# Weighing with the values ahead of the third part of a step's fill, in a two-layer hybrid decoder step

## The chip, the cores and the metric

The kernel runs on one core of a Trainium2 chip. The metric is the device time of one execution in microseconds (us). TensorE is called PE here, VectorE DVE, ScalarE ACT, GpSimd POOL and SyncE SP. Each engine works off its own instructions in order, and they wait for one another through semaphores.

## What is computed

One step of a decoder trunk with two layers, for a prompt of 1024 rows and 8 sample rows of width 1024. Per layer, cut to what matters here:

```python
h = rms_norm(x, norm1_g);  proj = h @ w_in          # columns: pool 512 | q 512 | k 512 | v 512
q, k = rope(q), rope(k)                             # 4 heads, two components of 64 each; v is 128 wide
s = einsum(q, k) * 64 ** -0.5                       # two score matrices a head, causal
p = softmax(s);  a = p[0] - lam * p[1]
o = einsum(a, v)                                    # 'weighing with the values'
attn = rms_norm(o, subln_g) * (1 - lam_init)
x = x + concat(pool_mixer(u), attn) @ w_out
x = x + conv_gated_ffn(rms_norm(x, norm2_g))
```

The 8 sample rows attend to 1024 cached positions each, in pages that a table names, and to their own key and value. A last RMS norm gives the outputs; new keys, values and states are stored as well.

## The kernel before

Activations lie transposed, features on the partitions, 1032 columns (1024 prompt rows and 8 sample rows) in three tiles of 344. A large product is made of three matmuls per 128 x 128 block (high part times high part, low times high, high times low). PSUM has eight banks; `claim(pe, name, b)` makes PE wait until the last use of bank b has been freed, and `freed(eng, name)` makes an engine wait for the freeing of one named use.

The attention of a layer is a loop over four heads (L725), and each head has eight steps (L734), one per block of 128 query rows, in the order 7, 0, 6, 1, 5, 2, 4, 3 (`ORDER`). Step s of a head holds, on PE:

- `scores` of the next step (L556 to L562), into banks 2 to 5; DVE reduces them to maxima (`maxima`, L1842), ACT takes two exponentials (`exps`, L1327 and L1330), and DVE forms their weighted difference (`combine`, L1850 to L1858), whose products have tiny ones (L1850, L1853: one element per partition) and one wide one (L1856).
- `turn_p` (L570), one or two rounds: the step's weights are transposed into bank 6, and ACT copies them to `a_T` (`take_p`, L1345).
- the fill: matmuls of a large product that are cut into portions. In heads 0 to 2 it is the projection of the next head's k, q and v (L477), nine slices of 24 matmuls, and `FILL` says how many matmuls a step holds; in head 3, the fourth, it is the output projection (L495) in slices of 21, with `FILL_OUT`. A step's fill comes in three parts (`part` matmuls twice, then the rest); in step 0 of head 3 the whole fill is the third part. The fill's slices go to banks 0 and 1 in turn. ACT copies a finished slice out (`take_k`, `take_q`, `take_v`, L1241), and behind the last slice of k or q it issues four DMAs that swap halves for the rotation (`rotate`, L1257). The slice that ends in a step's third part is copied late in ACT's step. The last slice of q ends with the sixth of the eight matmuls of step 4's third part.
- `turn_out` of the step before (L592): the normalised output rows are transposed, through bank 6.
- special work: step 0 turns the values (banks 7 and 6), step 4 turns the sample rows' scores (L614, L618; banks 7, 6, 7) and in heads 0 to 2 the next head's keys (`turn_k`, L531; banks 6 and 7, copied by ACT in `store_k`, L1290), step 5 forms the sample weights (L624, bank 6, behind a softmax of ACT, L1372, and DVE's `soft_weights`, L1904 to L1907), steps 6 and 7 weigh the sample rows' value pages (`sample_values`, L638, bank 7, copied by ACT, L1380); step 7 of heads 0 to 2 also spreads the next head's sample queries over the partitions (L542, bank 6). In step 7 `sample_out` (L646 to L649) sums the sample rows' output in a bank of the fill's ring.
- `weigh` (L581): two passes for each block of weights, into bank 7. It waits for bank 7, and for ACT's copies of the transposed weights.

Behind `weigh`, ACT takes squares of the rows (`square`, L1339; for the sample rows L1336), POOL adds and takes the reciprocal root (`rms`, L1024 and L1026), DVE multiplies (`normalise`, L1868), and frees bank 7. These three stand near the beginning of the next step in their engines' order: ACT's `square` of a step stands behind the slice copies of that step's third part.

POOL also splits weights into their low parts (`split_lo`, L1006), issues the gathers of the cached pages (L1041) and multiplies the cached keys by the query (`k_product`, L1049), three at a time in steps 1 and 2; its `rms` of step 0 stands ahead of the three products of step 1. DVE sums these products (L1883). In head 3, step 0, ACT, DVE and POOL split the seven chunks of the mixed rows, for which the output projection waits.

Behind the heads each layer runs its feed-forward network (L810 and L833), which the change does not touch.

Of the kernel before, what the change touches and what calls it, by code (L numbers as in the profile page):

```python
# [62 lines left out]
def rounds(i):  # L63
    return [list(range(a, min(a + 4, i + 1))) for a in range(0, i + 1, 4)]


def third(s, counts):

    return 0 if counts is FILL_OUT and s == 0 else counts[s] // 3
# [66 lines left out]
def hybrid_decoder_kernel(nc, x_prompt, x_sample, cache_k, cache_v, state_pool, state_conv, page_table, norm1_g, w_in,  # L136
# [4 lines left out]
    with ExitStack() as ctx:  # L141
# [177 lines left out]
        def claim(pe, name, b):  # L319
            USE[name] = (b, USES[b])  # L320
            if USES[b]:
                pe.wait_ge(bank_free[b], USES[b])
            USES[b] += 1
            return b
# [10 lines left out]
        def freed(eng, name):  # L335
            b, n = USE[name]
            eng.wait_ge(bank_free[b], n + 1)
# [71 lines left out]
        def _(pe):  # L409
# [96 lines left out]
            def slices(l, items, banks):  # L506
                for kind, n, t in items:
                    yield from (in_slice if kind == "in" else out_slice)(l, n, t, next(banks))

            def take(fill, n):  # L510
                for _ in range(n):
                    next(fill, None)
# [21 lines left out]
            def small_k(it):  # L534
                b = claim(pe, ("ks", it), 6)
                pe.transpose(bank[0:8, b, 0:P], k_buf[it % 2][:, SEQ:T], ident).then_inc(bank_full[b], 1)
# [8 lines left out]
            def scores(it, s):  # L545
                i = ORDER[s]
                q, k = q_buf[it % 2], k_buf[it % 2]
                for c in range(2):
                    claim(pe, ("s", it, s, c), 2 + 2 * c)
                if s == 0:  # L550
                    pe.wait_ge(roped, it * 2 + 2)
                halves = [(2 + 2 * c, slice(c * HEAD_DIM, (c + 1) * HEAD_DIM)) for c in range(2)]
                for n, at in enumerate(range(0, i * P, 512)):
                    w = min(512, i * P - at)
                    for b, rows in halves:
                        pe.matmul(bank[:, b + n, 0:w], q[rows, i * P:(i + 1) * P], k[rows, at:at + w],  # L556
                                  start=True, stop=True)
                last = [bank[:, b + i // 4, (i % 4) * P:(i % 4 + 1) * P] for b, _ in halves]
                for c, (b, rows) in enumerate(halves):
                    pe.matmul(last[c], q[rows, i * P:(i + 1) * P], k[rows, i * P:(i + 1) * P], start=True, stop=False)  # L560
                for c, (b, rows) in enumerate(halves):
                    pe.matmul(last[c], mask[:, 0, :], mask[:, 1, :], start=False, stop=True  # L562
                              ).then_inc(bank_full[b], 1)

            def turn_p(it, s, r):
                b = claim(pe, ("p", it, s, r), 6)
                if r == 0:
                    freed(pe, ("s", it, s, 1))
                for n, i in enumerate(rounds(ORDER[s])[r]):
                    ins = pe.transpose(bank[:, b, n * P:(n + 1) * P], probs[s % 2][:, i * P:(i + 1) * P], ident)  # L570
                ins.then_inc(bank_full[b], 1)

            def weigh(it, s):
                b = claim(pe, ("o", it, s), 7)
                i = ORDER[s]
                if s == 0:
                    freed(pe, ("vt", it, 1))
                for r, blocks in enumerate(rounds(i)):
                    freed(pe, ("p", it, s, r))
                    for n, j in enumerate(blocks):  # L580
                        ins = pe.matmul(bank[:, b, 0:P], a_T[:, r, n * P:(n + 1) * P], v_tok[:, j, :],  # L581
                                        start=(j == 0), stop=(j == i))
                ins.then_inc(bank_full[b], 1)

            def turn_out(it, n):
                b = claim(pe, ("to", it, n), 6)
                if n == QT_N:
                    freed(pe, ("so", it))
                    pe.transpose(bank[:, b, 0:8], o_norm8, ident[0:8, 0:8]).then_inc(bank_full[b], 1)
                else:  # L590
                    freed(pe, ("o", it, n))
                    pe.transpose(bank[:, b, 0:P], o_norm, ident).then_inc(bank_full[b], 1)  # L592

            def turn_v(it, r, b):
                claim(pe, ("vt", it, r), b)
                l, h = it // N_HEADS, it % N_HEADS
                if r == 0:
                    freed(pe, ("g", l, U_V(h), NT - 1))
                for a in range(4):
                    i = 4 * r + a  # L600
                    ins = pe.transpose(bank[:, b, a * P:(a + 1) * P], v_T[:, i * P:(i + 1) * P], ident)
                ins.then_inc(bank_full[b], 1)

            def small_v(it):
                b = claim(pe, ("vs", it), 6)
                pe.transpose(bank[0:16, b, 0:P], v_T[:, SEQ:T + 8], ident).then_inc(bank_full[b], 1)

            def turn_sample_scores(it):
                for r in range(2):
                    b = claim(pe, ("ss", it, r), 7 - r)  # L610
                    if r == 0:
                        pe.wait_ge(k_red, (it + 1) * DEC_BATCH)
                    for a in range(4):
                        ins = pe.transpose(bank[0:16, b, a * P:(a + 1) * P], s_score[:, :, :, 4 * r + a], ident)  # L614
                    ins.then_inc(bank_full[b], 1)
                b = claim(pe, ("ss", it, 2), 7)
                pe.wait_ge(qk_done, it + 1)
                pe.matmul(bank[0:16, b, 0:1], comp8, ones[:, 0:1], start=True, stop=True).then_inc(bank_full[b], 1)  # L618
# [45 lines left out]
            for l in range(DEPTH):  # L664
# [47 lines left out]
                it = l * N_HEADS  # L712
# [12 lines left out]
                for h in range(N_HEADS):  # L725
                    it = l * N_HEADS + h
                    final = h == N_HEADS - 1
                    if final:
                        fill = slices(l, [("out", m, t) for m in range(KC) for t in range(NT)], banks)
                        counts = FILL_OUT  # L730
                    else:
                        fill = slices(l, [("in", u(h + 1), t) for u in (U_K, U_Q, U_V) for t in range(NT)], banks)
                        counts = FILL
                    for s in range(QT_N):  # L734
                        part = third(s, counts)
                        if s + 1 < QT_N:
                            scores(it, s + 1)
                        elif not final:
                            scores(it + 1, 0)
                        turn_p(it, s, 0)  # L740
                        take(fill, part)
                        if len(rounds(ORDER[s])) > 1:
                            turn_p(it, s, 1)
                        take(fill, part)
                        if s >= 1:
                            turn_out(it, s - 1)
                        elif h:
                            turn_out(it - 1, QT_N - 1)
                        if s == 0:
                            turn_v(it, 0, 7)  # L750
                            turn_v(it, 1, 6)
                            small_v(it)
                            if h:
                                turn_out(it - 1, QT_N)
                        if s == 4:
                            turn_sample_scores(it)
                            if not final:
                                turn_k(it + 1, 0, 6)
                                turn_k(it + 1, 1, 7)
                        if s == 5:  # L760
                            sample_weights(it)
                        if s in (6, 7):
                            sample_values(it, s - 6)
                        if s == 7 and not final:
                            spread_q(it + 1, 0, 6)
                            spread_q(it + 1, 1, 6)
                            small_k(it + 1)
                        take(fill, counts[s] - 2 * part)
                        if s == 7:
                            sample_out(it, next(banks))  # L770
                        weigh(it, s)


                it = l * N_HEADS + N_HEADS - 1
# [1356 lines left out]
```

## Time and profile before

| | us |
|---|---|
| median of 3 runs | 2887.01 (2886.06 to 2888.28) |
| the profiled execution | 2887.58 |
| its span, first to last instruction | 2885.7 |
| PE busy | 2596.9 (90%) |
| DVE busy | 1535.2 (53%) |
| POOL busy | 820.8 (28%) |
| ACT busy | 744.3 (26%) |
| chain that ended last: PE L810 and L833 (feed-forward) | 33% and 18% |
| chain: PE L477 and L495 (the fills, and the projections ahead of the heads) | 5% and 5% |

The granted clock of PE is 0.941 of full speed over the span. Times below are counted from the first instruction of the profiled execution. In brackets behind a row of a timeline stands how long the engine was idle before it, and which engine's which line ended that.

### The profile page before, as it was taken

What the parts mean: (1) busy time and instruction counts of PE and PEld (TensorE: products, weight loads), DVE (VectorE), ACT (ScalarE), POOL (GpSimd) and SP (SyncE); (2) the same over time, 40 slices, a digit from 0 to 9 for tenths busy, and PEclk for the clock granted to TensorE, in tenths of its full rate; (3) what the DMA queues carried; (4) which work ended last, traced back from release to release, by engine and by line L of the source; (5) the groups of instructions that cost most, each with busy time, mean ns of one, the idle gap of its engine ahead of it and who ended that gap; (6) DMA issues with size and microseconds to landing.
All of it is one profiled execution on the core that took longest, in us unless ns stands there. A gap on an engine that the chain in (4) does not pass through costs nothing.

```text
span 2885.7 us, 41322 instructions
## 1 busy us (share of the span) xinstructions
PE 2596.9 (90%) x16556; PEld 2424.5 (84%) x16556; DVE 1535.2 (53%) x1903; ACT 744.3 (26%) x1409; POOL 820.8 (28%) x543
## 2 busy tenths in 40 slices
PE   6888777898999999999987888869899999999996
PEld 5777766888999999999886766758799999999996
DVE  5564764545445545455564664743654444554545
ACT  3223333232111121111132333332421111112112
POOL 1243553422222222222121553553222222222220
PEclk8889888999999999999998889889999999999997
DMA  3323344211111111111112343342011111111101
GB/s 122 121 93 120 109 139 132 90 45 45 44 44 44 48 52 47 44 45 51 47 55 89 106 144 117 106 138 89 29 45 44 44 44 44 44 47 50 50 30 59
DMA packets 78360, 205.96 MB, mean 71 GB/s; under 512 B 9146, under 2 KB 31100, under 8 KB 77994
## 3 DMA queue, kind: packets, MB, share of 16 engines
q1 hardware_dynamic: 35230, 112.92, 11.5%
q0 software_dynamic: 18496, 67.58, 7.2%
q10 hardware_dynamic: 24540, 24.15, 2.9%
q8 instruction: 67, 1.10, 0.2%
q14 instruction: 27, 0.22, 0.0%
HBM read 176.63 MB, written 19.98 MB: 68 GB/s over the span
## 4 chain that ended last, share of the span: by engine, by line
PE 72%; DVE 15%; ACT 5%; issue 2%; DMA 2%; POOL 2%; ACTq 1%; DVEq 0%; POOLq 0%
PE bank L810 33%; PE bank L833 18%; PE bank L477 5%; PE bank L495 5%; DVE stat L1850 4%; PE bank L581 2%; DVE parts_b L1883 1%; PE bank L638 1%; DVE stat L1842 1%; DMA arena<-in_cache_v,idx 1%; PE bank L556 1%; DVE arena L1702 1%; DVE arena L1856 1%; PE bank L862 1%; DVE arena L1810 1%
## 5 line engine op out<-in xcount | busy, mean ns | idle before, releaser
L1128 POOL TENSOR_TENSOR w_lo<-w_raw,w_hi 128x1024 fp32r<-128x1024 f32 x126 | 310.1, 2461 | 1157.4 <-ACT w_hi L1538 1157.4
L2040 DVE TENSOR_TENSOR resid<-bank,resid 128x1032 f32<-128x1032 f32 x336 | 414.2, 1233 | 91.7 <-PE bank L833 91.7
L810 PE MATMUL bank<-act_hi,w_hi 128*128 128x344 f32 x2016 | 433.6, 323 | 0.0
L810 PE MATMUL bank<-act_hi,w_lo 128*128 128x344 f32 x2016 | 427.6, 320 | 0.0
L810 PE MATMUL bank<-act_lo,w_hi 128*128 128x344 f32 x2016 | 426.5, 320 | 0.0
L810 PEld LDWEIGHTS bank<-act_hi,w_lo 128*128 128x128 f32 x2016 | 340.9, 189 | 0.0
L810 PEld LDWEIGHTS bank<-act_hi,w_hi 128*128 128x128 f32 x2016 | 336.1, 189 | 3.7
L810 PEld LDWEIGHTS bank<-act_lo,w_hi 128*128 128x128 f32 x2016 | 338.0, 188 | 0.0
L477 PE MATMUL bank<-act_hi,w_hi 128*128 128x344 f32 x672 | 236.6, 352 | 10.3 <-DVE arena L1791 10.3
L1006 POOL TENSOR_TENSOR w_lo<-w_raw,w_hi 128x1024 fp32r<-128x1024 f32 (+1 forms) x56 | 134.6, 2405 | 381.9 <-ACT w_hi L1167 381.7
L833 PE MATMUL bank<-gate_hi,w_hi 128*128 128x344 f32 x1008 | 235.6, 342 | 0.0
L477 PE MATMUL bank<-act_hi,w_lo 128*128 128x344 f32 x672 | 234.7, 349 | 0.0
L477 PE MATMUL bank<-act_lo,w_hi 128*128 128x344 f32 x672 | 229.4, 341 | 0.0
L833 PE MATMUL bank<-gate_hi,w_lo 128*128 128x344 f32 x1008 | 213.4, 320 | 0.0
L833 PE MATMUL bank<-gate_lo,w_hi 128*128 128x344 f32 x1008 | 213.2, 320 | 0.0
L1842 DVE TENSOR_REDUCE stat<-bank 128x1 f32<-128x128 f32 (+7 forms) x128 | 90.8, 751 | 228.0 <-PE bank L562 224.8
L833 PEld LDWEIGHTS bank<-gate_hi,w_hi 128*128 128x128 f32 x1008 | 154.7, 188 | 36.0 <-DVE resid L2040 24.1
L1550 ACT ACTIVATE arena<-arena 128x1024 f32<-128x1024 f32 x44 | 46.7, 1062 | 525.0 <-DVE arena L2023 525.0
L833 PEld LDWEIGHTS bank<-gate_hi,w_lo 128*128 128x128 f32 x1008 | 169.2, 188 | 0.0
L833 PEld LDWEIGHTS bank<-gate_lo,w_hi 128*128 128x128 f32 x1008 | 169.1, 188 | 0.0
L2031 DVE TENSOR_TENSOR arena<-bank,arena 128x1032 f32<-128x1032 f32 x44 | 54.3, 1234 | 207.4 <-PE bank L810 207.2
L2006 DVE COPY arena<-bank 128x16 f32<-128x16 f32 x44 | 7.7, 176 | 284.4 <-PE bank L817 284.3
(240 smaller groups left out, 4406.8 us busy)
## 6 DMA issues: line engine op xcount, KB each, us to landing
w_raw<-in_w_up SPq DMA_DIRECT2D x88, 512.0 KB
w_raw<-in_w_down SPq DMA_DIRECT2D x44, 512.0 KB
w_raw<-in_w_in SPq DMA_DIRECT2D x32, 512.0 KB
arena<-arena ACTq DMA_DIRECT2D x64, 129.0 KB, 2.6
out<-arena ACTq DMA_DIRECT2D x16, 512.0 KB, 3.2
w_raw<-in_w_out SPq DMA_DIRECT2D x16, 448.0 KB
mix_spill<-arena ACTq DMA_DIRECT2D x12, 516.0 KB, 3.1
w_raw<-mix_spill SPq DMA_DIRECT2D x12, 516.0 KB
```

The lines of the kernel that those rows point to most:

```text
L477: ins = pe.matmul(bank[:, b, 0:TW], w_of(w, l, n, k), x[:, k, cols(t)], start=(k == 0 and m == 0), stop=(k == KC - 1 and m == 2))
L495: ins = pe.matmul(bank[:, b, 0:TW], w_of(w, l, U_O + m, c), x[:, c, cols(t)], start=(c == 0 and a == 0), stop=(c == KC - 2 and a == 2))
L581: ins = pe.matmul(bank[:, b, 0:P], a_T[:, r, n * P:(n + 1) * P], v_tok[:, j, :], start=(j == 0), stop=(j == i))
L810: ins = pe.matmul(grp(u[0])[:, t, :], w_of(w, l, n, k), x[:, k, cols(t)], start=(k == 0 and n_ == 0), stop=(k == KC - 1 and n_ == 2))
L833: ins = pe.matmul(grp(u[0])[:, t, :], w_of(w, l, n, m), x[:, cols(t)], start=(n_ == 0), stop=(n_ == 2))
L1006: pool.tensor_tensor(w_lo[:, slot, 0:width], w_raw[:, r % SLOTS, 0:width], w_hi[:, slot, 0:width].bitcast(F32), ALU.subtract).then_inc(w_l ...
L1128: pool.tensor_tensor(w_lo[:, slot, :], w_raw[:, r % SLOTS, 0:1024], w_hi[:, slot, :].bitcast(F32), ALU.subtract).then_inc(w_lo_done, 1)
L1550: act.activation(gate[:, 0:SEQ], conv_c[:, 0:SEQ], ACT.Silu)
L1842: dve.tensor_reduce(stat[:, s % 2, c:c + 1], flat(b)[:, 0:width], AX_X, ALU.min).then_inc(att_bias, 1)
L1850: step(dve.tensor_tensor(st[:, 2:3], st[:, 4:5], neg_lam[it // N_HEADS], ALU.mult))
L2031: dve.tensor_tensor(tiles(gate), grp(u[0]), tiles(gate), ALU.mult).then_inc(fg_free[u[0]], 1)
L2040: dve.tensor_tensor(tiles(resid[:, m, :]), grp(u[0]), tiles(resid[:, m, :]), ALU.add).then_inc(fg_free[u[0]], 1)
```

## The change

In the loop over the steps, PE's call of `weigh` moves from behind the third part of the fill (and, in step 7, behind `sample_out`) to ahead of it. No other engine's order changes.

```diff
                             spread_q(it + 1, 0, 6)
                             spread_q(it + 1, 1, 6)
                             small_k(it + 1)
+                        weigh(it, s)
                         take(fill, counts[s] - 2 * part)
                         if s == 7:
                             sample_out(it, next(banks))
-                        weigh(it, s)
```

## Rows read from the trace of the kernel before

**Rows 1.** Page, chain that ended last: shares of the span by engine
```profile
PE 72%; DVE 15%; ACT 5%; issue 2%; DMA 2%; POOL 2%; ACTq 1%; DVEq 0%; POOLq 0%
```
**Rows 2.** Line L581 (weigh): what its engine's idle time before it waited for (us, times)
```profile
  issue: 1.8, 8
```
**Rows 3.** Chain of waits in the second head (286 to 345): start, us, what
```profile
289.18 5.80 DVE stat L1850
...
331.59 0.61 ACT arena L1290
...
333.97 0.35 ACT arena L1241
334.41 0.51 ACTq L1257
...
337.78 0.87 ACT arena L1327 x2
```
**Rows 4.** Timeline of POOL, second head, steps 0 and 1: start, us, engine, line
```profile
283.57 2.35 POOL L1006 TENSOR_TENSOR w_lo<-w_raw,w_hi 128x1024 fp32r<-128x1024 f32 x1 [5.61 <-ACT w_hi L1167]
285.87 0.20 POOL L1024 TENSOR_TENSOR stat<-stat 128x1 f32<-128x1 f32 x1
...
287.93 7.03 POOL L1049 TENSOR_TENSOR arena<-arena 128x1024 f32<-128x1024 f32 x3
```
**Rows 5.** Timeline of PE, second head: end of step 1, step 4, step 5
```profile
296.59 0.76 PE L556 MATMUL bank<-arena 64*128 64x128 f32 x4 [3.62 <-DVE arena L1856]
...
333.65 1.77 PE L581 MATMUL bank<-arena 128*128 128x128 f32 x12
...
341.62 0.91 PE L624 MATMUL bank<-small,arena 16*128 16x8 f32 x7 [1.11 <-DVE small L1907]
```
**Rows 6.** Timeline of PE, second head, step 7
```profile
364.90 3.59 PE L638 MATMUL bank<-arena 128*1 128x128 f32 x64 [3.12 <-DMA arena<-in_cache_v,idx]
...
370.23 1.12 PE L542 MATMUL bank<-arena,con 128*128 128x512 f32 x2 [0.69 <-ACT arena L1320]
...
372.47 0.32 PE L477 MATMUL bank<-act_hi,w_hi 128*128 128x344 f32 x1
...
373.09 0.31 PE L477 MATMUL bank<-act_hi,w_lo 128*128 128x344 f32 x1
...
374.33 1.16 PE L581 MATMUL bank<-arena 128*128 128x128 f32 x8
```
**Rows 7.** Timeline of ACT, second head, step 6
```profile
354.06 0.28 ACT L1380 ACTIVATE con<-bank 128x128 f32<-128x128 f32 x1 [1.58 <-PE bank L638]
```
**Rows 8.** Timeline of POOL, second head, steps 6 and 7
```profile
354.30 1.68 POOL L1041 DMA_INDIRECT arena<-in_cache_v,idx  x1 [5.26 <-PE bank L638]
...
375.98 0.18 POOL L1024 TENSOR_TENSOR stat<-stat 128x1 f32<-128x1 f32 x1 [2.46 <-ACT arena L1339]
```
**Rows 9.** Timeline of ACT, first head, step 4
```profile
230.71 0.60 ACT L1290 ACTIVATE arena<-bank 128x512 f32<-128x512 f32 x1 [0.26 <-PE bank L531]
...
232.99 0.43 ACT L1241 ACTIVATE arena<-bank 128x344 f32<-128x344 f32 x1
```
**Rows 10.** Timeline of PE, first head, step 4
```profile
232.34 1.50 PE L581 MATMUL bank<-arena 128*128 128x128 f32 x12
```
**Rows 11.** Timeline of PE, fourth head, steps 0 and 1
```profile
486.70 0.62 PE L495 MATMUL bank<-act_hi,w_hi 128*128 128x344 f32 x1 [2.73 <-DVE act_lo L1919]
...
498.95 3.15 PE L581 MATMUL bank<-arena 128*128 128x128 f32 x16
...
514.23 0.66 PE L495 MATMUL bank<-act_hi,w_hi 128*128 128x344 f32 x1 [6.31 <-DVE resid L1913]
```
**Rows 12.** Timeline of DVE, fourth head, step 1
```profile
506.28 5.91 DVE L1850 TENSOR_TENSOR stat<-stat,lam 128x1 f32<-128x1 f32 x1
```
**Rows 13.** Stretches: busy us (count) of PE, PEld, DVE, ACT, POOL; granted clock; DMA
```profile
228.40:231.80 3.40, 3.10 (x13) 3.10 (x14) 1.21 (x1) 1.49 (x4) 0.00 (x0) 0.50 0.02 5
324.00:334.20 10.20, 6.93 (x30) 5.85 (x31) 4.29 (x10) 5.76 (x14) 1.27 (x2) 0.50 0.25 79
```

## Prediction: what the change does to the time

> **What bounds the kernel now.** I read the chain that ended last, by engine: 72% of it is PE, 15% DVE, 5% ACT [rows 1]. The change touches the eight heads' steps alone, so I then read the matmul of the weighing by its source line: PE sat idle before it for 1.8 us in all, in 8 places [rows 2]. The weighing waits for nothing today, so nothing can be won at its own place; what an earlier one gives must come through its readers (ACT's square, POOL's root, DVE's normalising), and what it costs through what it meets sooner.
>
> The chain inside one head (the second of the first layer) shows two stretches that set the pace. At the end of step 1 DVE's one-element product L1850 lasts 5.80 us [rows 3]; it ends with POOL's three products of cached keys (L1049, from 287.93 for 7.03 us) [rows 4], and PE meanwhile waits 3.62 us for the next scores [rows 5]. In steps 4 and 5 the chain is ACT's: the second copy of turned keys (L1290), later the copy of q's last slice (L1241), four DMA issues that rotate q (L1257), the exponentials (L1327), then DVE, then PE's sample weights (L624) at 341.62, for which PE has stood 1.11 us [rows 5].
>
> **The change part by part.** No instruction is added or removed. In 64 steps the third part of the fill (6 to 12 matmuls in a layer's first three heads, 18 to 26 in its fourth) and the weighing trade places, so PE's work is the same and only waits move.
>
> *The weighing's two waits, met sooner.* It needs ACT's copy of the turned weights out of bank 6, and bank 7. turn_out, which stands ahead of it in both kernels, claims bank 6 and so has waited for that copy; in the first head of a layer, at step 0, the turned values do the same. Cost nothing. Bank 7 was last used by the previous weighing, whose normalising turn_out also waits for: nothing in steps 1, 2, 3 and 5. In step 0 the small turn of the values has waited for the last copy out of both banks; in step 7 of the first three heads two later copies by ACT lie between. Three places are left where bank 7 has just been filled: step 4 (the keys of the next head, in the fourth head the sample scores), step 6 (the sample values), and step 7 of the fourth head.
>
> *Step 4 of the first three heads: the stall.* PE's last turn of keys ends as ACT's L1290 starts at 331.59; that ends 0.61 later, at 332.20 [rows 3]. PE, which now runs eight fill matmuls there, would stand until some 332.25: 0.7 us. The same pattern (PE, a 512-wide copy by ACT, PE on the same bank) stands in step 7 with 0.69 us [rows 6]. Queued behind the weighing on PE are those eight fill matmuls, and ACT waits for the sixth of them.
>
> *Step 4: the late slice.* ACT now takes q's last slice at 333.97, right behind its softmax, because PE had finished it under that cover. Afterwards the fill comes behind stall and weighing. Second head: PE is at its lower clock level (granted 0.50, which is 1.2 GHz) until 334.2 [rows 13]; a pass of the weighing takes 3.15/16 = 0.197 us there [rows 11] and 1.50/12 = 0.125 at the upper level [rows 10]. From 332.25, ten passes end at 334.2 and two more at 334.45. The sixth fill matmul starts 5 x 0.155 later (four starts from 372.47 to 373.09, [rows 6]) and lasts 0.32, so ACT starts at 335.6, 1.6 us late. The four issues and the exponentials follow back to back on ACT, with 0.1 us of slack to PE's own turns: 1.5 us at L624. First head: bank free at 230.71 + 0.60 = 231.31 [rows 9]; the lower level ends at 231.8 [rows 13]; so the weighing ends at about 233.05 and the slice at 234.15, where ACT took it at 232.99: 1.2 us. Three heads have the long stretch of lower clock, three the short one: 3 x 1.5 + 3 x 1.2 = 8.1 us. Bounds: nothing, if the sample weights are held by something else; and 0.7 + 1.77 = 2.5 us a head (the stall and the whole weighing [rows 5]), 15 us. I take 8.1, because the chain of the trace runs through this very copy. It is not given back in the head: L624 is what PE waits for, and what follows is timed from it.
>
> *Step 6, first three heads.* PE ends the sample values when ACT's copy L1380 starts, 354.06, for 0.28 us [rows 7]: a stall of 0.4 us. But POOL issues the last four value pages from the end of the same matmuls (354.30, [rows 8]), and PE then waits 3.12 us for them in step 7 [rows 6]. The 0.4 goes into that wait: nothing; if this cover were gone, 6 x 0.4 = 2.4 us.
>
> *Fourth heads.* Step 6 and step 7 have the same stall with no page wait behind: 0.4 each. Step 4 waits for a copy of one column behind a 512-wide one: between 0.4 and 0.7, I take 0.6. Sum 1.4 a layer, 2.8 us; bounds 0 and 4. In step 0 the weighing moves ahead of 18 fill matmuls that wait for chunks of the mixed rows: its 3.15 us go into the wait of 2.73 us ahead of the first of them and the next one [rows 11]. PE then reaches the next scores some 3 us sooner, but waits again until 514.23, 6.31 us today [rows 11], for DVE, whose L1850 again lasts 5.91 us [rows 12] under POOL's products. POOL's chain there starts from its own splitting of weights, not from the square. Gain nothing.
>
> *The gains through the square.* In step 0 POOL's root starts at 285.87, while its own splitting of weights (283.57 + 2.35 = 285.92) ends [rows 4]; behind steps 1, 2 and 3 it likewise follows POOL's preceding instruction at once. An earlier square waits there. POOL does stand idle for the square behind step 4, but there the square follows ACT's DMA issues and not the weighing [rows 3], and behind step 7 (375.98, 2.46 us idle [rows 8]). In step 7 the weighing comes sooner by eight fill matmuls and the sample's sum, but on ACT the square stands behind the copy of the last value slice, which the weighing's 1.16 us [rows 6] now delays. Net 0.2 us a head, 4 heads that it helps (in the fourth heads step 0 is bound by the turned weights): 0.8 us.
>
> Sum: 8.1 + 2.8 - 0.8 = +10.1 us. The profiled execution took 2887.58 us (span 2885.7); 2897.7 on that footing. The median of the runs, 2887.01, lies 0.57 lower: 2897.1.
>
> One rule of the Trainium skill speaks otherwise. SBUF — State Buffer, Who interferes with whom, says that a VectorE instruction with two SBUF inputs and a GpSimd one that reads SBUF exclude each other for one whole instruction, and that the order of issue decides. The trace agrees on the exclusion, but L1850 outlasts three POOL products (5.80 us against 7.03/3 = 2.34 each). By the trace's form the fourth heads gain nothing; by the rule's they could, which is the third rival.
>
> **Rivals.**
> 1. *The wait is hidden after all.* L624 waits 1.11 us in the second head; if it were held by the softmax's sum and not by the late slice, the 0.7 us stall would drown in it. For: that wait exists [rows 5]. Against: the chain passes through L1241. Time: 2887.0 + 2.8 - 0.8 = 2889.0.
> 2. *The clock falls more often.* Each head's step 4 or 5 holds a stretch at 1.2 GHz today [rows 13], after PE had stood still; longer waits may add one per head. A stretch of 3.4 us at half pace loses 1.7 us: 6 x 1.7 on top, 2907.3. For: L624's wait grows to about 2 us. Against: fill follows at once.
> 3. *Not slower: DVE gets ahead of POOL in the fourth heads.* The scores of step 2 come 3 us sooner there; if that lets DVE's L1850 and the products behind it pass before POOL's three, PE's wait of 6.31 us goes, in two layers: 10.1 - 12.6 = -2.5, 2884.5. It decides if the sums of ACT's exponentials reach DVE before POOL starts, which it does some time before L1850's 506.28 [rows 12]. Against: DVE's reductions of those scores and both exponentials must still come first, and the first product alone is not enough.
> 4. *The root does start sooner*, because the square is what holds POOL: ten fill matmuls, 1.55 us, off the wait behind step 1 of six heads: 10.1 - 9.3 = 0.8, 2887.8. Against: POOL has no idle time before it [rows 4].
>
> That the change does nothing is excluded: the order of instructions on PE is written out by hand.
>
> **How the numbers follow.** Chances: forecast 0.62 (its own range 2892 to 2902), rival 1 0.17, rival 2 0.11, rival 3 0.06, rival 4 0.04. What this kernel's measurement can tell from no change is about 0.2%, 5.8 us: faster is below 2881.2, slower above 2892.8. Slower: the forecast without its lowest edge and rival 2, 0.70. Same: rivals 1, most of 3 and 4, and that edge, 0.23. Faster: rival 3 with more than two waits saved, or a chain I have not seen, 0.07. The range runs from 2887.5, just under rival 1, to 2904, short of rival 2's full price.
>
> **What would show it.** Right: in step 4 a new wait of about 0.7 us before L581 on ACT's L1290; L1241 in that step directly behind the fill and not behind the softmax; L624's wait up from 1.11 to about 2 us; a 0.4 us wait before L581 in step 6, and L638's 3.12 us shorter by as much; L1850 still 5.8 us. Wrong: no wait at L581, L624 unmoved against the turned keys, or a shorter L1850 in the fourth heads.

## The result, and the profile after

The changed kernel took 2906.36 us (median of 4 runs, 2903.36 to 2910.96) beside 2886.53 us for the kernel before (4 runs, 2884.08 to 2888.28): a ratio of 1.0071, 95% interval 1.0053 to 1.0088, or +15 to +25 us. It is slower, as forecast, but by about twice the +10.1 us that the sum gave. A second measurement (the repeat among the experiments) gave 1.0048, interval 1.0029 to 1.0067, or +8 to +19 us. The profiled execution after took 2905.41 us; its span is 2903.5, where before it was 2885.7: +17.8.

The chain of the profile after, shares by engine, against [rows 1]: TensorE's share falls by two points and "issue" takes three.

```profile
PE 70%; DVE 15%; issue 5%; ACT 4%; POOL 2%; DMA 2%; ACTq 1%; DVEq 0%; POOLq 0%
```

First, what the weighing (L581) waits for now, from TensorE's waits in the kernel after (engine, line, what it waited for: us in total, times, longest). Of before there was nothing to wait for [rows 2].

```profile
PE bank L638 <- DMA arena<-in_cache_v,idx: 17.0, 6, 3.3
...
PE bank L624 <- DVE small L1907: 15.2, 8, 2.2
...
PE bank L581 <- ACT arena L1290: 4.1, 6, 0.7
...
PE bank L581 <- ACT con L1380: 3.2, 8, 0.4
...
PE bank L581 <- ACT arena L1368: 1.2, 2, 0.6
...
PE bank L581 <- ACT parts_b L1380: 0.8, 2, 0.4
```

The same view of the kernel before has, of these, only the two that are not the weighing's:

```profile
PE bank L638 <- DMA arena<-in_cache_v,idx: 17.5, 6, 3.6
...
PE bank L624 <- DVE small L1907: 12.3, 8, 2.3
```

The four new waits are 9.3 us, each in the place and of the size that was forecast (0.69, 0.40, 0.6, 0.4 us). So the stalls are not where the forecast fell short.

Second, step 4 of the first and the second head on TensorE, after (start, us, line, idle before it and what ended it), to be held against [rows 5, 10]:

```profile
230.79 2.93 PE L581 MATMUL bank<-arena 128*128 128x128 f32 x12 [0.69 <-ACT arena L1290]
243.03 1.92 PE L624 MATMUL bank<-small,arena 16*128 16x8 f32 x16 [1.93 <-DVE small L1907]
...
335.49 2.93 PE L581 MATMUL bank<-arena 128*128 128x128 f32 x12 [0.69 <-ACT arena L1290]
...
347.00 2.06 PE L624 MATMUL bank<-small,arena 16*128 16x8 f32 x16 [2.19 <-DVE small L1907]
```

The twelve matmuls of the weighing last 2.93 us where they lasted 1.50 and 1.77 us. ScalarE in the same two places, against [rows 3, 9]:

```profile
230.14 0.60 ACT L1290 ACTIVATE arena<-bank 128x512 f32<-128x512 f32 x1 [0.26 <-PE bank L531]
...
235.47 0.46 ACT L1241 ACTIVATE arena<-bank 128x344 f32<-128x344 f32 x1 [2.96 <-PE bank L477]
...
334.84 0.60 ACT L1290 ACTIVATE arena<-bank 128x512 f32<-128x512 f32 x1 [0.26 <-PE bank L531]
...
339.44 0.46 ACT L1241 ACTIVATE arena<-bank 128x344 f32<-128x344 f32 x1 [2.23 <-PE bank L477]
```

From the end of L1290 to the copy of q's last slice (L1241) it is now 4.73 and 4.00 us; before it was 232.99 - 231.31 = 1.68 and 333.97 - 332.20 = 1.77 us. ScalarE now waits for the fill (L477), as the forecast said.

Third, the length of the place. I measured it from the end of L1290 to the first L624, in the first three heads of both layers: six stretches. The view of stretches gives for each the busy time of PE, PEld, DVE, ACT and POOL, then the granted clock and the DMA share; the last line sums the six. Before:

```profile
231.31:240.54 9.23, 7.62 (x53) 6.66 (x52) 3.85 (x11) 4.25 (x11) 0.74 (x2) 0.97 0.44 114
332.19:341.63 9.44, 8.33 (x53) 7.36 (x52) 3.82 (x11) 4.44 (x11) 0.73 (x2) 0.89 0.43 112
...
sum 57.82, PE 48.60 PEld 42.82 DVE 23.07 ACT 25.77 POOL 4.42; mean PE 8.10 PEld 7.14 DVE 3.85 ACT 4.29 POOL 0.74
```

And after:

```profile
230.73:243.03 12.30, 10.32 (x54) 9.09 (x55) 3.86 (x11) 4.37 (x12) 0.74 (x2) 0.79 0.33 86
335.43:347.00 11.57, 9.33 (x55) 8.27 (x55) 3.86 (x11) 4.37 (x12) 0.73 (x2) 0.87 0.35 91
...
sum 72.07, PE 59.71 PEld 52.73 DVE 23.17 ACT 26.22 POOL 4.42; mean PE 9.95 PEld 8.79 DVE 3.86 ACT 4.37 POOL 0.74
...
225.80:235.90 10.10, 8.88 (x39) 7.21 (x36) 1.73 (x3) 4.46 (x9) 0.00 (x0) 0.50 0.18 54
```

The six places are 72.07 - 57.82 = 14.25 us longer, for which the forecast had 8.1. Of these, 11.1 us is busy time of TensorE (59.71 - 48.60). One to three more matmuls stand in each place, the fill that TensorE used to run while ScalarE copied: about 0.69 us a place, 4.1 us in all. The other 7 us of busy time is the clock. A stretch of length t and mean granted clock c, at two levels 1 and 0.50, holds 2t(1-c) at the lower level. Over the six stretches of each kernel that makes 9.3 us before and 26.3 us after. Seventeen microseconds more at half pace cost at most 8.5 us, as far as TensorE was busy in them, which leaves room for those 7. The last line shows the first head: the lower level lasts from 225.8 to 235.9 now, where it had ended at 231.8 [rows 13].

Fourth, the whole of the attention (from the first to the last L562, one stretch a layer). Columns: length, TensorE's busy time, clock, DMA. Before:

```profile
165.58:590.28 424.70, 339.40 (x2371) 0.88 0.36 114
1573.59:2000.62 427.03, 341.65 (x2371) 0.87 0.36 113
sum 851.73, PE 681.06; mean PE 340.53
```

After:

```profile
165.75:600.95 435.20, 344.59 (x2370) 0.87 0.35 111
1584.25:2017.54 433.29, 342.84 (x2370) 0.87 0.36 111
sum 868.49, PE 687.42; mean PE 343.71
```

The repeat of after, the sum:

```profile
sum 865.65, PE 684.67; mean PE 342.34
```

Nearly all of the loss lies here: +16.8 us of the 17.8, and +13.9 in the repeat (whose span was 2898.8, +13.1). In both, TensorE stands idle 10.3 to 10.4 us longer (868.49 - 687.42 = 181.1 and 865.65 - 684.67 = 181.0, against 170.7). What differs between the two executions is how much longer the same matmuls took: 6.4 and 3.6 us.

### The profile page after: what moved, and what is told of

It is laid out like the page before. It is cut to its first block, busy times and chain, and to the rows that moved or that the text cites. A ratio compares the mean times of both kernels' runs of the same rounds, so it can differ in the third digit from the quotient of the medians.

```text
span 2903.5 us, 41322 instructions
## 1 busy us (share of the span) xinstructions
PE 2602.4 (90%) x16556; PEld 2419.0 (83%) x16556; DVE 1538.4 (53%) x1903; ACT 741.7 (26%) x1409; POOL 821.0 (28%) x543
## 3 DMA queue, kind: packets, MB, share of 16 engines
q1 hardware_dynamic: 35230, 112.92, 11.3%
## 4 chain that ended last, share of the span: by engine, by line
PE 70%; DVE 15%; issue 5%; ACT 4%; POOL 2%; DMA 2%; ACTq 1%; DVEq 0%; POOLq 0%
PE bank L810 33%; PE bank L833 18%; PE bank L477 5%; PE bank L495 5%; DVE stat L1850 4%; PE bank L581 2%; DVE parts_b L1883 2%; DVE stat L1842 1%; DMA arena<-in_cache_v,idx 1%; DVE arena L1702 1%; PE bank L862 1%; PE bank L638 1%; PE bank L556 1%; DVE arena L1810 1%; DVE arena L1856 1%
## 5 line engine op out<-in xcount | busy, mean ns | idle before, releaser
L477 PE MATMUL bank<-act_hi,w_hi 128*128 128x344 f32 x672 | 234.0, 348 | 10.3 <-DVE arena L1791 10.3
L477 PE MATMUL bank<-act_hi,w_lo 128*128 128x344 f32 x672 | 232.0, 345 | 0.0
L477 PE MATMUL bank<-act_lo,w_hi 128*128 128x344 f32 x672 | 227.1, 338 | 0.0
```

The costliest lines, as they stand in the source:

```text
L477: ins = pe.matmul(bank[:, b, 0:TW], w_of(w, l, n, k), x[:, k, cols(t)], start=(k == 0 and m == 0), stop=(k == KC - 1 and m == 2))
```

## The experiments

Each run is given against the kernel before on the same chip, as a ratio with its 95% interval and in microseconds (ratio less 1, times 2887). The stretches at step 4 are those of the third view above. What the expectations call the root is the softmax of the sample rows (VectorE's L1904 to L1907), for which TensorE waits at L624.

**Where the loss is: step 4 alone, and all but step 4.** The weighing stays early in one set of steps and goes back in the other:

```
+ early = s == 4 and not final        # first kernel
+ early = final or s != 4             # second kernel
+ if early: weigh(it, s)
  take(fill, counts[s] - 2 * part)
  ...
+ if not early: weigh(it, s)
```

> The weighing is put ahead of the third part at step 4 of the first three heads of a layer alone (six places); every other step keeps the order of before. Theory (step 4 holds nearly all of the loss: a standstill, a late slice, and a low clock that outlasts them): +14 us against before, 11 to 17, and in each of the six places the root of the single-row softmax comes 1.7 to 3.1 us later, with the weighing at the lower clock and 2.9 us long. Rival (each of the 64 steps pays a little, step 4 its forecast share): +8 us or less.

> The weighing is ahead of the third part in every step except step 4 of the first three heads of a layer, where the order of before stands. Theory: what is left is the fourth heads' stalls, 2.8 us by the forecast, less the gain at the end of a head: +1 to +5 us against before, about +3. Rival (each step pays a little): +11 us or more.

Measured: 1.0045 (1.0027 to 1.0063), +13.0 us, for step 4 alone; 1.0012 (0.9999 to 1.0024), +3.5 us, for all the rest. In the first, the root came 2.0 to 2.9 us later in the six places (72.85 us in sum against 57.82), every weighing 2.93 us long. The two add up to 16.5, between the two measurements of the whole change (13.9 and 20.5). So six of the 64 steps hold nearly all of the loss. What the other 58 cost, -0.3 to +6.9 us by the interval, agrees with the forecast's 2.8 - 0.8 = 2.0 and can't be told from nothing.

**The late slice without the standstill, and the standstill without the late slice.**

```
  # four of eight ahead               # standstill only
+ take(fill, 4)                     + freed(pe, ("kt", it + 1, 1))
  weigh(it, s)                        take(fill, rest)
+ take(fill, rest - 4)                weigh(it, s)
```

> Order of before, but at step 4 of the first three heads four of the third part's eight matmuls stand ahead of the weighing and four behind it. q's last slice still waits for the whole weighing (its last two matmuls are behind it), but TensorE has matmuls to run while ScalarE copies the second half of k, so the standstill of 0.69 us is filled. Theory (the clock stays low because of the standstill): the weighing runs in 1.5 to 1.8 us instead of 2.93, and the time is +7 us against before, 4 to 10. Rival (the late slice alone costs what is lost, whatever the clock): +12 us or more.

> Order of before, with one added wait: at step 4 of the first three heads TensorE waits for ScalarE's copy of the second half of k before it begins the third part, the standstill of the changed kernel with no instruction moved. Theory (the standstill keeps the clock at its lower level for some us): more than its own six times 0.69 us = 4.1 us; +7 us against before, 4.5 to 12, with the granted clock at 0.50 from the standstill to well into the next step. Rival (a standstill costs at most itself, and the loss is the order's): 0 to +4 us.

Measured: 1.0030 (1.0017 to 1.0042), +8.7 us, for the split; 1.0030 (1.0016 to 1.0045), +8.7 us, for the standstill. Both times fall into the theory's intervals, both by a reason that is only half its own. The stretches of the split kernel (first, second, sum):

```profile
231.27:242.01 10.74, 8.55 (x53) 7.49 (x52) 3.85 (x11) 4.37 (x12) 0.74 (x2) 0.89 0.38 98
332.46:342.13 9.67, 7.48 (x52) 6.42 (x52) 3.86 (x11) 4.36 (x11) 0.73 (x2) 0.99 0.42 109
...
sum 64.03, PE 50.79 PEld 44.41 DVE 23.14 ACT 26.14 POOL 4.42; mean PE 8.47 PEld 7.40 DVE 3.86 ACT 4.36 POOL 0.74
```

and of the kernel with the standstill alone (first, sum):

```profile
231.06:242.57 11.51, 10.34 (x54) 9.26 (x55) 3.83 (x11) 4.57 (x12) 0.74 (x2) 0.77 0.36 91
...
sum 70.15, PE 63.19 PEld 56.27 DVE 22.92 ACT 27.39 POOL 4.43; mean PE 10.53 PEld 9.38 DVE 3.82 ACT 4.57 POOL 0.74
```

Three rows of its TensorE, second head, at the added wait (here L1292 is the line that the others have as L1290):

```profile
333.46 0.65 PE L477 MATMUL bank<-act_hi,w_hi 128*128 128x344 f32 x1 [0.69 <-ACT arena L1292]
333.91 0.49 PE L477 MATMUL bank<-act_hi,w_lo 128*128 128x344 f32 x1
334.20 0.49 PE L477 MATMUL bank<-act_lo,w_hi 128*128 128x344 f32 x1
```

Without a standstill the six places hold 13.7 us at the lower level, near the 9.3 of before; with it 34.2 us, though not one instruction has moved. So a wait of 0.69 us here is followed by some 4 us more at 1.2 GHz (3 to 6 by the place), and the places grow by 12.3 us for a wait of 4.1. All kernels of this section divide in the same way: where TensorE does not stand still behind L1290 (before and seven others) the six places hold 7.2 to 15.9 us at the lower level, and where it does (both executions of the changed kernel and four others) 21.6 to 34.2.

The kernel does not lose in full what its six places lose, though. The attention of the kernel with the standstill alone:

```profile
sum 859.09, PE 681.23; mean PE 340.61
```

It is 7.4 us longer than before (851.73), and all of that is idle time: TensorE's busy time is that of before (681.06), so the slower matmuls of the six places were made up for in other steps of this execution.

The expectation of the split also said that its weighing would run in 1.5 to 1.8 us, and in five of the six places it took 2.5 to 2.8 (1.50 in the second head alone): the stretch at the lower level reaches into this place in the kernel before too [rows 13], and an earlier weighing meets more of it.

**Neither.** The weighing stands ahead of the last two matmuls of the third part, so q's slice is done and TensorE has work while ScalarE copies (`take(fill, 6)`, `weigh`, `take(fill, rest - 6)`).

> Order of before, but at step 4 of the first three heads the weighing stands ahead of the third part's last two matmuls alone, which belong to the next slice; q's last slice is finished ahead of it as before. Neither late slice nor standstill. Theory: nothing left to lose, within 3 us of before. Rival (a weighing anywhere ahead of the fill's end at step 4 loses, because it delays the fill): +5 us or more.

Measured: 0.9992 (0.9980 to 1.0004), -2.3 us. Its six places:

```profile
sum 59.34, PE 51.74 PEld 45.35 DVE 22.96 ACT 26.49 POOL 4.42; mean PE 8.62 PEld 7.56 DVE 3.83 ACT 4.42 POOL 0.74
```

An early weighing as such costs nothing that the runs can tell (-5.8 to +1.2 us), although the six places hold 15.9 us at the lower level here, 6.5 more than before.

**Filling the standstill.** With the repeat of the changed kernel beside it:

```
  turn_k(it + 1, 1, 7)
+ idle(pe, 0)
+ for _ in range(4):
+     pe.matmul(bank[:, 0, 0:P], ident, ident, start=True, stop=True)
```

> The changed kernel once more, beside the two that follow on the same chip: +15 to +25 us against before, as measured, +19.9.

> The changed kernel with four extra 128x128 matmuls on TensorE at step 4 of the first three heads, behind the turned keys and ahead of the weighing, into a bank of the fill that is free; nothing reads them. They take 4 x 0.197 us at the lower level, about the 0.69 us that TensorE stands there, so the order and ScalarE's copy are the same and only the standstill is filled with work. Theory (the standstill is what lengthens the stretch at the lower clock): the stretch from the copy to the sampled row's weights loses 2 to 4 us of lower clock in each of the six places and the time falls by 5 to 10 us, to +10 to +15 against before. Rival (the low stretch is there anyway, and the loss is the order's): no change, +17 to +22.

Measured: 1.0048 (1.0029 to 1.0067), +13.9 us, for the repeat, a little under its expectation; 1.0044 (1.0031 to 1.0057), +12.7 us, for the filled kernel. The stretches of the repeat (sum) and of the filled kernel (first, sum), then the sum of the filled kernel's attention:

```profile
sum 73.35, PE 61.95 PEld 54.55 DVE 23.16 ACT 26.21 POOL 4.43; mean PE 10.32 PEld 9.09 DVE 3.86 ACT 4.37 POOL 0.74
...
232.59:244.23 11.64, 9.45 (x60) 8.39 (x59) 3.86 (x11) 4.37 (x12) 0.74 (x2) 0.90 0.35 90
...
sum 67.65, PE 54.47 PEld 48.11 DVE 23.18 ACT 26.20 POOL 4.42; mean PE 9.08 PEld 8.02 DVE 3.86 ACT 4.37 POOL 0.74
...
sum 874.86, PE 696.74; mean PE 348.37
```

In the place the mechanism did what the theory said: the lower level is down to 9.7 us, as before the change, and the six places are 67.65 us long, 5.7 less than in the repeat (73.35). But the filling came out too long. The trace has two matmuls for each of the four, eight in a place, here in the second head (L762 is the added line):

```profile
337.53 1.92 PE L762 MATMUL bank<-con 128*128 128x128 f32 x8
339.24 2.26 PE L581 MATMUL bank<-arena 128*128 128x128 f32 x12
```

They take 1.54 to 1.92 us and not the 0.8 of the expectation, so that the weighing begins 0.5 to 0.9 us behind ScalarE's copy, where it began 0.05 us behind it in the repeat: some 4.4 us in all that the test itself puts on.

The time did not follow the place: +12.7 lies in the theory's interval, but only because the repeat came out low too, and against the repeat it is 1.2 us less. With intervals of some 4 and 5 us to either side, a gain at the lower end of the expected 5 to 10 us is not excluded. In the profiled execution the attention is 9.2 us longer than in the repeat (874.86 against 865.65), although the six places are 5.7 us shorter, so its other steps were some 15 us longer. TensorE's busy time is 12.1 us more; the 48 extra matmuls are 9.8 of that, and as the other matmuls of the six places took less, those of other steps took more, at a mean granted clock of 0.86 and 0.87 against 0.87 and 0.88. This execution is the slowest of the five (2908.80 us, median 2902.26), so how much of those 15 us is the kernel's and how much the execution's stays open.

**How the lateness reaches the end.** Two moves around the root of the sampled row: ScalarE's four DMA issues (L1257) go behind the exponentials of step 5, on the order of before and on that of after; and the sample weights (L624) go behind the third part of step 5, with ScalarE's copy of them behind the slices, on either order too.

```
  exps(*after)
+ if s == 5 and not final: rotate(it + 1, 1, q_buf[(it + 1) % 2])   # ScalarE
  ...
- if s == 5: sample_weights(it)                                      # TensorE
  take(fill, counts[s] - 2 * part)
+ if s == 5: sample_weights(it)
```

> Order of before; the four DMA issues that follow the copy of q's last slice on ScalarE at step 4 (the rotation's, 0.5 to 0.6 us each in the rows) come one exponential later, behind the two exponentials of step 5. Theory (at step 4 the path to the root runs through ScalarE's queue, copy, four issues, exponentials): the exponentials come 1.2 to 2.4 us sooner in six heads: -8 us against before, -14 to -3. Rival (TensorE's own order sets the step, and ScalarE's issues lie beside it): within 2 us of before.

> The changed kernel with the same move of ScalarE's four DMA issues behind the exponentials of step 5. Theory (of the 2.5 us that a head loses at step 4, the late slice acts through the four issues that stand between it and the exponentials): it takes back 1.5 to 2.4 us a head, 9 to 14 us in all, and stands at +2 to +9 against before (the standstill and the low clock of the weighing stay). Rival (the weighing at the low clock sets the step by itself): +15 us or more, little taken back.

> Order of before, but at step 5 the sampled row's weights (TensorE's wait for the root, 1.1 to 2.3 us in the six heads and 1.56 in the two fourth heads) are made behind the third part of the fill and not ahead of it, and ScalarE takes them behind the slices. Theory (that wait is what turns a late step 4 into time): the third part covers it: -9 us against before, -14 to -4. Rival (the wait comes back at the weighing or at the next step, where ScalarE or VectorE are late in turn): within 3 us of before.

> Both moves on the order of before: the four DMA issues behind the exponentials of step 5, and the sampled row's weights behind the third part at step 5. Theory (both act on the one wait for the root, so they don't add): about what the better of the two gives, -9 us against before, -16 to -4. Rival (they act on different waits): the sum of the two, -16 us or lower.

> The changed kernel with e8's move: the sampled row's weights at step 5 behind the third part, and ScalarE takes them behind the slices. e8 has taken 22 us off the order of before; the question is what the change costs on top of that. Theory (most of the change's loss at step 4 reaches the end through TensorE's wait for the root at step 5, so what covers that wait covers the loss; TensorE's own standstills and slow matmuls stay): the change costs 4 to 12 us here and not 20, the kernel stands at -18 to -10 against before. Rival (TensorE pays the loss in step 4 itself, whatever it waits for later): the change costs its 18 to 20 us again, -4 to 0.

Measured: the issues behind, on before: 0.9981 (0.9966 to 0.9995), -5.5 us, within the theory's interval, but not by its path. Over the six places the exponentials begin only 0.35 us sooner in all, and the places are hardly shorter than the 57.82 us of before. ScalarE without the four issues waits 1.46 us in each place for TensorE's turned weights (L570) instead. Places (sum), then ScalarE in the second head:

```profile
sum 57.43, PE 50.74 PEld 44.93 DVE 22.92 ACT 26.68 POOL 4.43; mean PE 8.46 PEld 7.49 DVE 3.82 ACT 4.45 POOL 0.74
...
338.41 0.49 ACT L1345 ACTIVATE arena<-bank 128x384 f32<-128x384 f32 x1 [1.46 <-PE bank L570]
```

So in the kernel before, ScalarE's issues and TensorE's own order end at about the same time, and where the 5.5 us come from is not shown; in the profiled execution they are mostly shorter busy time of TensorE over the attention (674.56 against 681.06 us). On after: 1.0037 (1.0023 to 1.0052), +10.7 us. There the places do shrink, from 72.07 to 66.16 us, and the exponentials begin as much sooner. So in the changed kernel the issues were on the path, but it gets back only 3 to 10 us by their move, between the theory's interval and the rival's: the exponentials now wait for TensorE instead. ScalarE of that kernel, second head:

```profile
341.60 0.46 ACT L1241 ACTIVATE arena<-bank 128x344 f32<-128x344 f32 x1 [2.96 <-PE bank L477]
...
344.37 0.49 ACT L1345 ACTIVATE arena<-bank 128x384 f32<-128x384 f32 x1 [2.05 <-PE bank L570]
344.84 0.80 ACT L1327 ACTIVATE arena<-bank,stat 128x640 f32<-128x640 f32 x1
```

The sample weights behind the third part, on before: 0.9923 (0.9906 to 0.9941), -22.2 us; together with the issues 0.9922 (0.9907 to 0.9938), -22.5 us. This is the version that beats both kernels, by 0.8% the one before and by 1.2 to 1.5% the one after. The two moves don't seem to add, as the theory had it: the sum would be -27.7, just outside the interval of both together (-27 to -18), and so the rival of the sum fails, if narrowly, although its bound of -16 is passed. But the gain is larger than any expectation and than the wait that is covered (12.3 us). TensorE in the second head of the first of these two kernels:

```profile
338.45 1.95 PE L624 MATMUL bank<-small,arena 16*128 16x8 f32 x16
```

and the sum of its attention (both layers):

```profile
sum 828.44, PE 669.02; mean PE 334.51
```

L624 has no wait for the root any more. Idle time over the attention fell by 11.3 us (828.44 - 669.02 = 159.4 against 170.7), and the same matmuls took 12.0 us less (669.02 against 681.06), at a mean granted clock of 0.90 and 0.88 in the two layers against 0.88 and 0.87: fewer standstills, fewer stretches at the lower level.

The change on top of that: 0.9969 (0.9957 to 0.9981), -9.0 us, where its base stands at -22.2. It costs 13 us there, by the difference of the two, between the theory's 4 to 12 and the rival's 18 to 20; with both intervals it may be 7 to 19. On the order of before it cost 13.9 and 20.5, so the covered wait takes up 1 to 7 us, which the runs can't tell from nothing, and the larger part is paid on TensorE in step 4 itself. The places show it, without the change and with it:

```profile
sum 59.62, PE 59.62 PEld 53.97 DVE 23.17 ACT 28.24 POOL 4.43; mean PE 9.94 PEld 8.99 DVE 3.86 ACT 4.71 POOL 0.74
...
sum 71.65, PE 71.32 PEld 65.06 DVE 23.17 ACT 28.95 POOL 4.44; mean PE 11.89 PEld 10.84 DVE 3.86 ACT 4.83 POOL 0.74
```

They are 12.0 us longer, nearly all of it TensorE's busy time. It agrees with the changed kernel's own trace: of the 14.25 us by which L624 comes later, only 2.9 are a longer wait at L624 (15.2 against 12.3), and TensorE itself arrives there 11.4 us later.

## Why the prediction was right and wrong

Right, step by step: the weighing waits in step 4 behind L1290 (0.69 us in six places, 0.7 forecast), in step 6 behind L1380 (0.40), in the fourth heads behind L1368 and the last L1380 (0.6 and 0.4). L1241 follows the fill and no longer the softmax. L624's wait in the second head rose from 1.11 to 2.19 us ("about 2"), and its sum over eight heads from 12.3 to 15.2. L638's wait in the second head fell from 3.12 to 2.56 us, by the stall and a little more, but its sum only from 17.5 to 17.0, and it is 16.9 to 18.7 us in kernels whose step 6 is that of before; so whether the wait took up the stall of step 6 is not shown, and at its full 2.4 us it is a term that I had put at nothing. L1850 in the second head lasts 6.08 us for the 5.80 of [rows 3]. The fourth heads gain nothing at the scores of step 2: TensorE waits 7.59 us there instead of 6.31 [rows 11], under an L1850 of 7.19 us instead of 5.91 [rows 12]. VectorE's product in the fourth head, after:

```profile
514.92 7.19 DVE L1850 TENSOR_TENSOR stat<-stat,lam 128x1 f32<-128x1 f32 x1
```

And TensorE's wait:

```profile
524.16 0.66 PE L495 MATMUL bank<-act_hi,w_hi 128*128 128x344 f32 x1 [7.59 <-DVE resid L1913]
```

Rival 3 is out by these, and rivals 3 and 4 by the second kernel of the experiments: with the gains of 12.6 or 9.3 us it would have stood at -7 or lower, and it stands at +3.5 (-0.3 to +6.9). Rival 1 is out by the six longer places.

Wrong: the step "the late slice", 8.1 us. Its order and its path were right; its size was read with the end of the lower clock taken over from the trace of before ("the lower level ends at 231.8", "until 334.2"). That end was the wrong thing to carry over, because the change puts a standstill just ahead of it. In the first head the slice was to come 2.84 us behind L1290 and came 4.73; in the second 3.40 was forecast and 4.00 came. In both all twelve passes ran at the lower level, and in the first the fill behind them too. The price of a pass there was a little low as well: the last 0.7 us of the row behind 3.15/16 = 0.197 ran at a granted clock of 1.00, and twelve passes wholly at 0.50 take 2.58 us from start to start, 0.215 each. Of the three heads that I had put down as the cheap ones (1.2 us), since their clock had been back at the upper level, two lost the most (12.30 - 9.23 = 3.07 and 12.31 - 9.54 = 2.77 us) and the third the least, 1.68. Summed, the term measured 14.25 us (15.5 in the repeat) for 8.1, about the upper bound that the prediction itself gave for it (15). It is near to rival 2, whose price was one more stretch at 1.2 GHz a head, after the longer wait at L624; the runs show the stretch that was there lengthened instead, behind the new standstill, where I argued "fill follows at once" against it: in the first head the fill did follow, and at 1.2 GHz. That rival 2's 2907.3 lies so near the measured 2906.36 is in part luck, for the repeat came out at 2900.00.

With 14.25 in place of 8.1 the sum is +16.2 us, and the profiled span gave +17.8. In the repeat the term is 15.5 and the span +13.1, so there some 4 us came back in other steps.

What stays open is how much of the lower clock in step 4 is a loss over the whole head. Filling the standstill took it away in its place and won no time that the runs can tell, the standstill alone left TensorE's busy time over the attention as it was, and the weighing with two matmuls behind it had 6.5 us more at the lower level in its places and was no slower. The idle time of TensorE grew by the same 10.3 to 10.4 us in both profiled executions of the changed kernel, while its slowed busy time differed (6.4 and 3.6 us). In these two the idle time is the steady part, 9.3 us of it in the four new waits; the clock's share differs from execution to execution.

## What to carry to other kernels

A forecast for a place where the engine has just stood still can't take the end of the low-clock stretch from the trace of before: price the work behind a new standstill at the lower level throughout, as the upper bound, and as the likelier case where the standstill is new. Before an instruction is moved ahead of filler work, look whether that filler was what covered a copy that the moved instruction waits for; leaving enough of the filler ahead (here six of eight matmuls) cost nothing that could be measured. And the wait that such a lateness runs into was worth more here than the change: filler put ahead of TensorE's wait for the sampled row's root took 22 us off.

## What the runs showed of the hardware

A standstill of 0.69 us, with no instruction moved, lengthened six stretches by 12.3 us: 128x344 matmuls started 0.29 us apart after it and 0.155 us at the upper level [rows 6]. Where TensorE stood still there, the six stretches held 21.6 to 34.2 us at the granted clock of 0.50, and where it did not, 7.2 to 15.9. And the lower level, taken out of the six places by 48 extra matmuls (from 31.4 us in the repeat to 9.7), came back in others, in the one execution of each that was profiled: the attention's mean granted clock was 0.86 and 0.87 in that kernel, 0.87 and 0.88 in the repeat. VectorE's one-element product L1850 again lasted until POOL's products of cached keys beside it were done: it took 7.62 us in the second head after, begun 0.59 us ahead of POOL's three products, which took 7.00 us, and ended with the third of them. VectorE:

```profile
304.35 7.62 DVE L1850 TENSOR_TENSOR stat<-stat,lam 128x1 f32<-128x1 f32 x1
```

POOL at the same time:

```profile
304.94 7.00 POOL L1049 TENSOR_TENSOR arena<-arena 128x1024 f32<-128x1024 f32 x3
```
